# Three of eight experts in 64-slot, two-pass form, alternating with five in 128-slot, three-pass form, in a two-layer decoder kernel

## What is computed

```python
logits = (xt @ w_router + b_router)             # 256 tokens, 8 experts
top_val, top_idx = lax.top_k(logits, 2)         # each token goes to 2 experts
gates = softmax(top_val)
hb = jax.nn.silu(xb @ w1[e]) * (xb @ w3[e])     # xb: the tokens of expert e; w1, w3: 1024 x 3584
yb = hb @ w2[e]                                 # w2: 3584 x 1024
out[token] += gate * yb
```

## Time and profile before

| | us |
|---|---|
| median of three runs | 1526.01 |
| span of the profiled execution (first to last instruction) | 1524.0 |
| experts' stage, end of the first w1 product to the first matmul of the drain | 946.2 |
| TensorE busy in the span | 1505.0 |
| VectorE busy | 1306.8 |
| ScalarE busy | 989.3 |
| weights read in the experts' stage: 336 chunks of 1 MB | 352 MB |

### The profile page before, as it was taken

One profiled execution on the slowest core, in us unless ns is written; L12 is line 12 of the kernel. 1 busy time (PEld: TensorE's weight loads), 2 busy tenths in 40 slices (PEclk: granted clock), 3 DMA queues, 4 the chain that ended last, 5 costly groups with the idle time before them and its releaser, 6 DMA issues.

```text
span 1524.0 us, 18849 instructions
## 1 busy us (share of the span) xinstructions
PE 1505.0 (99%) x7604; PEld 1270.3 (83%) x7604; DVE 1306.8 (86%) x1296; ACT 989.3 (65%) x894; POOL 73.7 (5%) x103
## 2 busy tenths in 40 slices
PE   9999999999999999999999999999999999999996
PEld 5799888788899988888888888888888888888885
DVE  6898889787778678999899898899899888998886
ACT  2773553345673577777677767776777677767774
POOL 5000000000000000000000000000000000000000
PEclk9999999999999999999999999999999999999998
DMA  9859679985546659999999999999999999999992
GB/s 374 340 204 353 244 260 401 361 332 212 195 165 243 216 196 358 381 373 386 378 372 389 393 360 386 385 368 379 386 381 368 394 378 361 397 386 363 408 379 100
DMA packets 74224, 506.88 MB, mean 333 GB/s; under 512 B 8337, under 2 KB 8465, under 8 KB 16658
## 3 DMA queue, kind: packets, MB, share of 16 engines
q1 hardware_dynamic: 69986, 490.91, 82.9%
q0 software_dynamic: 4144, 14.70, 3.2%
HBM read 498.74 MB, written 6.83 MB: 332 GB/s over the span
## 4 chain that ended last, share of the span: by engine, by line
PE 93%; DVE 3%; DMA 2%; ACT 1%; SPq 1%; issue 1%; DVEq 0%; ACTq 0%
PE ps L1655 29%; PE ps L1657 29%; PE ps L1656 29%; PE ps L2184 2%; DMA raw<-in_w_first_dram 2%; PE ps L1880 1%; PE ps L1863 1%; ACT hi L570 1%; DVE lo L1029 1%; PE ps L2116 0%; DVE lo L1058 0%; PE ps L1870 0%; PE ps L1994 0%; SPq L399 0%; SPq L373 0%
## 5 line engine op out<-in xcount | busy, mean ns | idle before, releaser
L1058 DVE TENSOR_TENSOR lo<-raw,hi 128x2048 fp32r<-128x2048 f32 x336 | 751.0, 2286 | 46.0 <-ACT hi L586 45.8
L586 ACT ACTIVATE hi<-raw 128x2048 fp32r<-128x2048 f32 x336 | 626.4, 1916 | 58.7 <-PE ps L1657 55.4
L1655 PE MATMUL ps<-hi,hT_hi 128*128 128x512 f32 (+3 forms) x1232 | 480.7, 390 | 4.2 <-DVE hT_lo L1082 1.9
L1657 PE MATMUL ps<-hi,hT_lo 128*128 128x512 f32 (+3 forms) x1232 | 473.7, 384 | 0.0
L1656 PE MATMUL ps<-lo,hT_hi 128*128 128x512 f32 (+3 forms) x1232 | 473.3, 384 | 0.0
L1655 PEld LDWEIGHTS ps<-hi,hT_hi 128*128 128x128 f32 x1232 | 231.4, 188 | 52.4 <-issue 5.5
L1657 PEld LDWEIGHTS ps<-hi,hT_lo 128*128 128x128 f32 x1232 | 231.2, 188 | 45.3
L1656 PEld LDWEIGHTS ps<-lo,hT_hi 128*128 128x128 f32 x1232 | 231.6, 188 | 41.9
L1655 PE MATMUL ps<-hi,bT_hi 128*128 128x512 f32 (+1 forms) x576 | 223.9, 389 | 0.0
L1657 PE MATMUL ps<-hi,bT_lo 128*128 128x512 f32 (+1 forms) x576 | 222.9, 387 | 0.0
L1656 PE MATMUL ps<-lo,bT_hi 128*128 128x512 f32 (+1 forms) x576 | 222.8, 387 | 0.0
(11 more groups left out here) (303 smaller groups left out, 1213.9 us busy)
## 6 DMA issues: line engine op xcount, KB each, us to landing
raw<-in_moe_w_dram SPq DMA_DIRECT2D x336, 1024.0 KB, 7.5
raw<-in_w_ada_dram SPq DMA_DIRECT2D x40, 1024.0 KB, 6.9
raw<-in_w_fd_dram SPq DMA_DIRECT2D x11, 1024.0 KB, 7.4
raw<-in_w_ga_dram SPq DMA_DIRECT2D x8, 1024.0 KB, 6.1
raw<-in_w_gb_dram SPq DMA_DIRECT2D x8, 1024.0 KB, 5.0
raw<-in_w_ab_dram SPq DMA_DIRECT2D x8, 1024.0 KB, 5.2
raw<-in_w_o_dram SPq DMA_DIRECT2D x8, 1024.0 KB, 6.8
raw<-in_w_fg_dram SPq DMA_DIRECT2D x8, 1024.0 KB, 6.7
```

The source lines that it names most:

```text
L586: act.activation(hi[:, (s - PLAIN) % NSPLIT, :], raw[:, r % NRAW, :], ACT.Copy).then_inc(hi_done, 1)
L1058: dve.tensor_tensor(lo[:, at, :], raw[:, r % NRAW, :], hi[:, at, :].bitcast(f32), ALU.subtract).then_inc(raw_done, 1)
L1655: pe.matmul(o, wh, mh, start=first, stop=False)
L1657: return pe.matmul(o, wl, mh, start=False, stop=last)
```

## The change

After the first expert (expert 0, always in a large item) the experts are ordered by their token count. The five first items are "large" (128 slots, three passes, as before); the last three, with the fewest tokens, are "small": 64 slots. In a small item the stationary operand holds the 64 tokens' high part in its columns 0 to 63 and the low part in 64 to 127, so that two matmuls (with `W_hi` and `W_lo`) do what three did; the product then has two rows for each token, and they are summed when the inner rows are turned: a matmul with `stack`, the identity above itself, 64 columns wide. This is done for the w1 and the w3 product apart, eight matmuls instead of four transposes, and silu and the product come after the turn, on 256 columns.

The 56 groups now form one list of units: 7 large, then small and large in turn (units 7 to 52 hold the 21 small ones; every fourth small one is followed by two large ones), then three large. With 44, 31 and 16 tokens in the small items and at most 125 in the large ones, no spare item is needed. Chunks stream in the order of the units; the two rings, and what they wait for, are as before. The first six units' spare VectorE time now also holds the ordering of the experts.

The core of the diff:

```diff
+LARGE = 5
+HALF_CAP = P // 2
+SMALL_AT = [7 + 9 * k // 4 for k in range((EXPERTS - LARGE) * NG)]
...
+            for n, (i, g) in enumerate(UNITS):
+                if g == 0 and i:
+                    sp.wait_ge(experts_ready, 1)
+                    expert[i] = sp.value_load(info[0:1, i:i + 1], min_val=0, max_val=EXPERTS - 1)
+                unit_loads(n, ("w1", "w3"))
+                if n:
+                    unit_loads(n - 1, ("w2",))
...
+            def scatter_rows(i):
+                f = FINISHED[i]
+                pool.wait_ge(m_yc, f)
+                rows_each = P if i < LARGE else HALF_CAP
...
+            def two(o, both, mh, ml, first, last):
+                pe.matmul(o, both, mh, start=first, stop=False)
+                return pe.matmul(o, both, ml, start=False, stop=last)
...
+                if SMALL[n]:
+                    pe.wait_ge(small_ready, 3)
+                    for z, src in enumerate((gate_s, up_s)):
+                        for c in range(4):
+                            at = z * 256 + c * HALF_CAP
+                            m = pe.matmul(ps[:, 2, at:at + HALF_CAP], src[:, c * P:(c + 1) * P], stack, start=True, stop=True)
+                else:
+                    for c in range(4):
+                        m = pe.transpose(ps[:, 2, c * P:(c + 1) * P], h_large[:, c * P:(c + 1) * P], ident[:, :])
```

A unit on ScalarE, in the order written (`b` is the unit's first chunk; VectorE's unit has the same form, with `small_hidden` and `small_lo`):

```diff
+                if n:
+                    moe_hi(b + 2)
+                if n in FINISH_AT:
+                    weighted_y(FINISH_AT[n])
+                moe_hi(b + 3)
+                if n:
+                    moe_hi(b + 4)
+                    (small_silu if SMALL[n - 1] else hidden_hi)(n - 1)
+                    moe_hi(b + 5)
+                    if SMALL[n - 1]:
+                        small_hi(n - 1)
...
+                if SMALL[n]:
+                    act.activation(gate_s, ps[:, 0, :], ACT.Copy).then_inc(m_silu, 1)
+                else:
+                    act.activation(h_large, ps[:, 0, :], ACT.Silu).then_inc(m_silu, 1)
...
+                moe_hi(after)
+                if SMALL[n]:
+                    up_done(n, "w3")
+                    act.activation(up_s, ps[:, 1, :], ACT.Copy).then_inc(m_up, 1)
```

More of the change, by code:

```diff
@@ L150, with spot @@
 GATES = [(l, v) for l, v in ADA if v in (G_M, G_F)]
-def spot(kind, g, half=1, first=False):
+def spot(kind, g, half=1):
     if kind == "w2":
@@ L171, in item_order, with units @@
     return out
-LAST = [(PER_ITEM - 2 + h, "w2", NG - 1, h, False) for h in range(2)]
+LAST = [(PER_ITEM - 2 + h, "w2", NG - 1, h) for h in range(2)]
 DRAIN = (7, 0, 1, 2)
+LARGE = 5
+HALF_CAP = P // 2
+UNITS_ALL = EXPERTS * NG
+SMALL_AT = [7 + 9 * k // 4 for k in range((EXPERTS - LARGE) * NG)]
+def units():
+    out, at = [], [0, 0]
+    for n in range(UNITS_ALL):
+        small = n in SMALL_AT
+        item, g = divmod(at[small], NG)
+        out.append((LARGE + item if small else item, g))
+        at[small] += 1
+    return out
@@ L178, with same_kind_before, unit_chunk, last_up_chunk @@
+ALL_ROWS = max(ROWS_OUT.values())
+def same_kind_before(order, i):
+    j = order.index(i)
+    kin = [o for o in order[:j] if (o >= LARGE) == (i >= LARGE)]
+    return kin[-1] if kin else None
+def unit_chunk(n, kind, half):
+    if kind == "w2":
+        n += 1
+    return max(6 * n - 2, 0) + {"w1": 0, "w3": 2, "w2": 4 if n < UNITS_ALL else 0}[kind] + half
+def last_up_chunk(i):
+    return unit_chunk(FINAL[i], "w3", 1)
 Y_BANK = (3, 5)
@@ L872, in item, with spare_item @@
[L872 to L882, removed]
+            def spare_item(i):
+                for h in range(2):
+                    spare_x(i, h)
+                item_hi(i, 0, 2)
+                at = [2]
@@ L888, in item @@
                 for g in range(NG):
[L889 to L892, removed]
+                    c = spot("w1", g)
                     upto_c(min(c + 2, PER_ITEM - 1))
@@ L923, in y_half @@
                                ACT.Square, scale=D ** -0.5, accum_out=ms[:, q:q + 1]).then_inc(sq_done, 1)
[L925 to L928, removed]
+            for h in range(2):
+                first_scaled(h)
+                for b in (2 * h, 2 * h + 1):
+                    first_high(b)
+            for n in range(UNITS_ALL):
+                unit(n)
+            act.activation(warm[:, :], warm[:, :], ACT.Sqrt)
             drain(EXPERTS - 1)
@@ L939, in _ @@
                     with act.If(spare > i - EXPERTS):
[L940 removed]
+                        spare_item(i)
                         drain(i)
@@ L1616, in last_residual @@
                                              ALU.mult, ALU.add).then_inc(o_done, 1)
-            item(0, 0, True, True)
-            for i in range(1, EXPERTS - 1):
-                item(i, i % 2, False, True)
-            item(EXPERTS - 1, 1, False, False)
+            first_x()
+            for n in range(UNITS_ALL):
+                unit(n)
             dve.wait_ge(gate_f_in, 16 * L)
@@ new lines, in unit_down @@
+            def unit_down(n, turn_next=False, last=False):
+                i, g = UNITS[n]
+                small = SMALL[n]
+                if g == 0:
+                    before_ = same_kind_before(FINISH + [END], i)
+                    if before_ is not None:
+                        pe.wait_ge(m_yc, FINISHED[before_])
+                    elif small:
+                        pe.wait_ge(idx_ready, 3)
+                pe.wait_ge(m_h, n + 1)
+                for half in range(2):
+                    wh, wl = moe_part(unit_chunk(n, "w2", half))
+                    order = [(cc, q) for cc in range(2) for q in range(2)]
+                    if last and half:
+                        order = [(cc, q) for q in range(2) for cc in range(2)]
+                    for cc, q in order:
+                        c = 2 * half + cc
+                        w = slice(cc * D + q * 512, cc * D + (q + 1) * 512)
+                        first, final = g == 0 and c == 0, g == NG - 1 and c == 3
+                        if small:
+                            m = two(ps[:, 6 + q, :], h_both[:, c, :], wh[:, w], wl[:, w], first, final)
+                        else:
+                            k = large_slots(n).start + c
+                            m = three(ps[:, 4 + q, :], bTh[:, k, 0:P], bTl[:, k, 0:P], wh[:, w], wl[:, w], first, final)
+                        if last and half and (cc, q) == (1, 0):
+                            m.then_inc(m_y0, 1)
+                    m.then_inc(used, 1)
+                    if turn_next and half == 0:
+                        unit_turn(n + 1)
@@ new lines, in unit @@
+            def unit(n):
+                i, g = UNITS[n]
+                if n:
+                    pe.wait_ge(m_silu, n)
+                unit_up(n, "w1")
+                if n:
+                    unit_turn(n - 1)
+                if n == 1:
+                    slot_rows(0)
+                if n in ROWS_AT:
+                    slot_rows(ROWS_AT[n])
+                if n in TURN_AT:
+                    turn_rows(*TURN_AT[n])
+                if (i, g) == (END, 3):
+                    pe.wait_ge(m_xf, 2 * EXPERTS - 2)
+                    for t in range(T):
+                        m = pe.transpose(ps[:, 3, t * P:(t + 1) * P], r4[:, 256 + t * P:256 + (t + 1) * P], ident[:, :])
+                    m.then_inc(m_gt, 1)
+                unit_up(n, "w3")
+                if n == 1:
+                    pe.wait_ge(ov_ready, 1)
+                if n:
+                    unit_down(n - 1, turn_next=n == UNITS_ALL - 1)
```

598 lines of the change are left out of this document (395 added, 203 removed).

## The result

The changed kernel takes 1459.84 us, the median of four runs (1459.62 to 1461.42); the kernel before took 1526.17 us on the same chip. The ratio is 0.957, with a 95% interval of 0.955 to 0.958: 66 us less, where 61.5 to 62 were forecast (1464). The span of the profiled execution is 1458.2 us.

What follows compares the result with a forecast made beforehand. The DMA was to bound units 7 to 53: 724 + 8 + 3 = 735 us against 798.5, 63.5 less; with 2 us for ordering, 1526.0 - 61.5 = 1464 us. Forecast 1452 to 1484 (0.63); 8 in 10: 1447 to 1494.

Steps and rivals of the forecast that it cites:

- TensorE's price: Small unit on TensorE: 48 matmuls for 72, turn 1.5 us, 12.4 us against 16.8; 1433 us if TensorE stayed the bound.
- The DMA's need: Units 7 to 53: 282 chunks at 2.49 us (421 GB/s) plus 22 us of scatters and gathers, 724 us.
- The DMA engines want most.: Units 7 to 53: DMA needs 724 us, TensorE 703, VectorE 683, so the DMA sets the stretch.
- The 8 us added for the ring: Six `raw` buffers leave 1.1 us for a chunk waiting for ScalarE; 8 us added over units 7 to 53.
- The gathers: Units 15 and 18: gathers with one unit until TensorE turns their rows; 0 to 3 us wait each, 3 together.
- The ordering of experts: Units 0 to 6: some 25 more operations in VectorE's idle time, 0 to 5 us, taken as 2.
- loads of SP: SP's register loads and run-time addresses hide in its waits for a free buffer, costing nothing.
- The end: Last small item's two scatters and read, 37.2 us, fit the 39 us before the drain; nothing, uncovered 1 to 5 us.
- (1): Rival: TensorE or VectorE, not the DMA, sets the mixed stretch; 1433 to 1452 us, chance 0.13.
- (2): Rival: the DMA engines give little more than now, under 400 GB/s; 1484 to 1522 us, chance 0.18.
- (3): Rival: a small unit's chain stands still behind late chunks, making the kernel slower; 1569 us, chance 0.03.
- (4): Rival: a spare item runs after all; 119 us more, 1583 us, chance 0.01.

Runs made afterwards that it cites:

- three_pass_small: The changed kernel with the small units' third pass given back (first pass run twice), in the new order of units: 1553.9 us.
- light_lo: The changed kernel with VectorE making `lo` for only the first 1024 of 2048 columns of each expert chunk: 1450.8 us.
- half_loads: The changed kernel with only the first 1024 of 2048 columns of each expert chunk loaded, all engine work kept: 1456.8 us.

## Why the prediction was right, and where it was not

**TensorE's price.** 24 matmuls less per small unit hold: 48 at 0.2267 us. The turn was mis-sized, "Sixteen instructions are 1.44 us by the first and 1.76 by the second; I take 1.5": it is 1.8 by `three_pass_small` and 1.7 by the timeline, at the upper end or above it, so TensorE needs up to 703 + 21 x 0.33 = 710 us. With DMA and VectorE light, the stretch is 712.7 us and the time 1439.1, where my floor of 1433 and those 7 us give 1440.

**The DMA's need** stands: 724 us by count, 724.8 in `light_lo`, where the DMA is what is waited for. The changed kernel's stretch took 732.1, where I gave 735. Chunks take 9.1 us to land (7.5 before), as the row of 9.3 let expect. Two readings under it were generous: of the 40 single microseconds 18, not most, are at 400 or more, and in the earlier trace rows one slice of the stage has 358, not more. The 421 doesn't rest on them.

```profile
raw<-in_moe_w_dram SPq DMA_DIRECT2D x270, 1024.0 KB, 9.1
```

**The step that failed is "The DMA engines want most."** I compared sums of work: 724, 703 and 683 us, and took the largest. VectorE's 683 leave out that it stands still for ScalarE at fixed places of each unit; with those it needs about 30.1 us per pair, as `half_loads` shows, which is the DMA's 29.9 over again. TensorE stands at 29.5. Three limits within 0.6 us gave the same number that one did. The forecast's time was right and its reason only part of the story: that the chain's 729.4 us lay so near the 735 forecast from the DMA's need was luck. The 8 us added for the ring are isolated by no run; 732.1 - 724 - 3 leaves 5 for them, and `half_loads` shows that the chain alone asks for nearly all of these.

**The gathers** were forecast with 3 us; undoing their wait gives 2.1 in the stage. **The ordering of experts**, forecast with 2 us, shows as 1.4: from the first silu to unit 7 it takes 115.9 us against 114.5 for the same groups before. The **loads of SP**, nothing, hold. **The end** held: the last scatter's read was issued at 1425.48 and landed in 5.7 us, 11 us before the drain:

```profile
1404.63 2.79 POOL L660 DMA_INDIRECT rows_y<-r,scatter_row  x1 [120.16 <-ACT r L1014]
1414.62 2.81 POOL L660 DMA_INDIRECT rows_y<-r,scatter_row  x1 [7.19 <-DMA rows_y<-r,scatter_row]
1425.48 0.80 POOL L669 DMA_DIRECT2D r<-rows_y  x1 [8.05 <-DMA rows_y<-r,scatter_row]
```

**The rivals and the signs.** (1) asked for under 1452 us: not so, as the chain through VectorE and the DMA keep TensorE from its pace. (2) fell: 418 to 422 GB/s in whole slices. (3), the slower side, did not come: from 700 to 1400 us TensorE waits 6.7 us for the large units' low parts and not once for a small unit's. (4) did not come. Where the signs of the profile were listed, "ScalarE's `hi` waiting for DMA for tens of us" came true (24), and alone it would have been taken as proof of the DMA bound; a wait that short, beside two of 40 us, was no proof. The pair of 31.2 us came as the mean (732.1 over 47 units); but from one unit's w1 to the next a good pair had 16.9 and 13.2 us, more uneven than listed, and TensorE's 25 us of idle time were 11 in the trace.

What stays open: where in a unit the chain of VectorE and the ring would have to be cut. Neither a fifth `hi`/`lo` pair nor a seventh `raw` buffer was tried.

## What to carry to other kernels

When the bound engine gets less work, add up for the others not their busy time but their busy time with the waits that their order of instructions forces on them, and expect the next limits in a row: here three lay between 29.5 and 30.1 us per pair, and lifting one gave 3 or 9 us, two together 21. A stream can stand at its full rate and not be the only bound; a run that halves it tells. Before taking more matmuls away from an engine that begins to wait, look at its clock: work removed where it isn't fed can cost more than it saves.

## What was not expected of the hardware

- Removing 21 x 24 of TensorE's matmuls made the kernel 28 us slower (1487.8 against 1459.8). TensorE was half busy (1.99 and 2.04 us of 4), with gaps of 0.6 to 1.7 us each, the granted clock fell to 0.50, and the matmuls after it started every 0.43 us instead of 0.23 until it rose again. With the same matmuls and no lack of chunks the mean clock stayed at 0.997 (1343.1 us).
- Eight float32 matmuls of 64 columns, in 16 instructions, take 1.7 to 1.8 us, 0.11 each: as much as transposes of 128 columns, and more than the 0.09 of 4 columns.
- The rate of 421 GB/s that a backlog showed for 40 us before now stands in many slices of 36 us (418 to 422), and the mean over 730 us, with scatters and gathers in it, is 413 GB/s.
